# Decay sums of the state-space heads as scanned rows, laid over all partitions through a small DRAM table

## What is computed

```python
da = dtc * a.reshape(G, E)
acs = jnp.cumsum(da, axis=2).transpose(0, 1, 3, 4, 2)
seg = acs[..., :, None] - acs[..., None, :]
lmat = jnp.exp(jnp.where(tri, seg, -jnp.inf))
cb = jnp.einsum('bclgn,bcsgn->bcgls', cc, bc)
y_diag = jnp.einsum('bcgls,bcgels,bcsgep->bclgep', cb, lmat, xdt)
decay_states = jnp.exp(acs[..., -1:] - acs)
states = jnp.einsum('bclgn,bcgel,bclgep->bcgepn', bc, decay_states, xdt)
y_off = jnp.einsum('bclgn,bcgepn,bcgel->bclgep', cc, prev, jnp.exp(acs))
```

## Time and profile before

| what | us |
|---|---|
| median of 3 runs | 1007.55 |
| lowest and highest | 1007.19, 1009.74 |
| the profiled execution | 1008.01 |
| its span, first to last instruction | 1006.2 |
| mean granted PE clock, share of 2.4 GHz | 0.988 |

### The profile page before, as it was taken

One profiled execution on the slowest core, in us unless ns is written; L12 is line 12 of the kernel. 1 busy time (PEld: TensorE's weight loads), 2 busy tenths in 40 slices (PEclk: granted clock), 3 DMA queues, 4 the chain that ended last, 5 costly groups with the idle time before them and its releaser, 6 DMA issues.

```text
span 1006.2 us, 15135 instructions
## 1 busy us (share of the span) xinstructions
PE 962.0 (96%) x6561; PEld 876.1 (87%) x6561; DVE 644.7 (64%) x732; ACT 461.5 (46%) x553; POOL 59.4 (6%) x79
## 2 busy tenths in 40 slices
PE   6999989999999999999899999999899999999996
PEld 6999779999999899776699989997899888999884
DVE  5966895545455853565659778688677765455444
ACT  6456744443435355644454343445354434444342
POOL 2033000000000000120030000000000000000000
PEclk9999999999999999899999999999999999999999
DMA  8743466555564643212479999985455454565621
GB/s 259 242 131 126 159 196 218 180 184 193 175 202 128 188 147 111 84 43 85 153 279 329 387 310 343 306 320 194 172 179 179 145 183 163 176 201 170 204 87 42
DMA packets 122282, 190.52 MB, mean 189 GB/s; under 512 B 6566, under 2 KB 103080, under 8 KB 119144
## 3 DMA queue, kind: packets, MB, share of 16 engines
q1 hardware_dynamic: 115184, 156.94, 48.3%
q0 software_dynamic: 5616, 31.78, 8.6%
q10 hardware_dynamic: 1416, 0.83, 0.3%
HBM read 188.49 MB, written 1.05 MB: 188 GB/s over the span
## 4 chain that ended last, share of the span: by engine, by line
PE 79%; DVE 11%; ACT 6%; issue 2%; DMA 1%; DVEq 0%; ACTq 0%; POOL 0%
PE PS L562 15%; PE PS L564 15%; PE PS L563 15%; PE PS L569 9%; PE PS L570 9%; PE PS L571 9%; DVE lo L1559 4%; ACT hi L1130 2%; PE PS L695 1%; PE PS L660 1%; DMA raw<-even_w_in 1%; ACT hid L1417 1%; DVE r L1629 1%; PE PS L1014 1%; DMA sq<-norm_gains 1%
## 5 line engine op out<-in xcount | busy, mean ns | idle before, releaser
L1559 DVE TENSOR_TENSOR lo<-raw,hi 128x2048 fp32r<-128x2048 f32 (+2 forms) x150 | 336.0, 2259 | 163.8 <-ACT hi L1130 163.5
L562 PE MATMUL PS<-x_hi,hi 128*128 128x256 f32 x1320 | 376.1, 285 | 2.1 <-DVE x_lo L1756 2.1
L564 PE MATMUL PS<-x_hi,lo 128*128 128x256 f32 x1320 | 373.9, 283 | 0.0
L563 PE MATMUL PS<-x_lo,hi 128*128 128x256 f32 x1320 | 373.2, 283 | 0.0
L1130 ACT ACTIVATE hi<-raw 128x2048 fp32r<-128x2048 f32 (+2 forms) x150 | 277.8, 1879 | 8.5 <-DMA raw<-even_w_in 6.4
L562 PEld LDWEIGHTS PS<-x_hi,hi 128*128 128x128 f32 x1320 | 251.9, 191 | 4.5 <-DVE lo L1559 2.4
L563 PEld LDWEIGHTS PS<-x_lo,hi 128*128 128x128 f32 x1320 | 252.7, 191 | 1.7 <-issue 0.5
L564 PEld LDWEIGHTS PS<-x_hi,lo 128*128 128x128 f32 x1320 | 251.8, 191 | 0.0
L569 PE MATMUL PS<-hi,hid_hi 128*128 128x512 f32 x352 | 141.5, 402 | 6.0 <-DVE lo L1559 5.5
L570 PE MATMUL PS<-lo,hid_hi 128*128 128x512 f32 x352 | 139.8, 397 | 0.0
L571 PE MATMUL PS<-hi,hid_lo 128*128 128x512 f32 x352 | 139.1, 395 | 0.0
(11 more groups left out here) (276 smaller groups left out, 833.5 us busy)
## 6 DMA issues: line engine op xcount, KB each, us to landing
raw<-ffn_w_gate SPq DMA_DIRECT2D x22, 1024.0 KB, 5.4
raw<-ffn_w_up SPq DMA_DIRECT2D x22, 1024.0 KB, 5.4
raw<-ffn_w_down SPq DMA_DIRECT2D x22, 1024.0 KB, 5.0
raw<-mlp_w_in SPq DMA_DIRECT2D x16, 1024.0 KB, 5.6
raw<-mlp_w_out SPq DMA_DIRECT2D x16, 1024.0 KB, 5.0
sq<-ada_w POOLq DMA_DIRECT2D x12, 1024.0 KB, 6.2
r<-ada_w POOLq DMA_DIRECT2D x12, 1024.0 KB, 6.7
raw<-sc_w_in SPq DMA_DIRECT2D x12, 1024.0 KB, 5.3
```

What stands on the lines that cost most here:

```text
L562: pe.matmul(dst, wh, hi, start=start, stop=False, skip_group_check=True)
L563: pe.matmul(dst, wh, lo, start=False, stop=False, skip_group_check=True)
L564: return pe.matmul(dst, wl, hi, start=False, stop=stop_, skip_group_check=True)
L1559: dve.tensor_tensor(split_view("lo", c), split_view("raw", c), split_view("hi", c).bitcast(F32), ALU.subtract)\
```

## The change

The running sums are made by DVE, with two scans of 16 x 128 along the rows of the decays, into `small[0:16, 3, :]`. POOL writes these 16 rows to a DRAM tensor `acs_rows` (16 KB) and reads each block's half back onto all 128 partitions, 16 pieces of 512 bytes for each partition, into `r` (block 0) and `lnrow` (block 1). PE's `small` turns the sums instead of the decays, the products L795, L796 and L818 are gone, and DVE and ACT take the sums from the two tiles. The rows of the first layer norm are loaded after the last reader of `lnrow`. The row product of chunk 13 no longer waits for the readers of the PSUM banks.

```diff
+        acs_rows = nc.dram_tensor("acs_rows", (HEADS, S), F32, kind="Internal").ap()
+        acs_all = (r_all[:, :].rearrange("p (h s) -> p h s", h=HEADS),
+                   lnrow[:, :, :].rearrange("p a (b s) -> p (a b) s", s=P))
...
             pool.wait_ge(sem("even_evac"), 1)
             pool.dma_start(pool_w_sb[:, :, :], A["pool_w"][0].rearrange("g c d -> c g d")).then_inc(sem("poolw_landed"), 16)
-            ln_rows("ln0")
+            pool.wait_ge(sem("acs_ready"), 2)
+            pool.dma_start(acs_rows[:, :], small[0:16, 3, :]).then_inc(sem("poolw_landed"), 16)
+            pool.wait_ge(sem("poolw_landed"), 32)
+            for j in range(2):
+                pool.dma_start(acs_all[j], acs_rows[:, j * P:(j + 1) * P].rearrange("(o h) s -> o h s", o=1)
+                               .to_broadcast([P, HEADS, P])).then_inc(sem("acs_landed"), 16)
             pool.wait_ge(sem("pad_zero"), 3)
...
+            pool.wait_ge(sem("seg_done"), 8)
+            pool.wait_ge(sem("eacs_done"), 4)
+            ln_rows("ln0")
             pool.wait_ge(*sig_at("ln0", "x", 4))
...
-                pe.wait_ge(sem("da_ready"), 1)
+                pe.wait_ge(sem("acs_ready"), 2)
...
-                        last = pe.transpose(PS[:, 0, o:o + 16], small[0:16, q, j * P:(j + 1) * P], ident[0:16, 0:16])
+                        last = pe.transpose(PS[:, 0, o:o + 16], small[0:16, 3 * q, j * P:(j + 1) * P], ident[0:16, 0:16])
...
-                    for c in range(2):
-                        pe.matmul(PS[:, 0, 64 + 16 * c:80 + 16 * c], triu, tok[:, c, 16:32], start=True, stop=True)
-                    pe.matmul(PS[:, 0, 96:112], ones[:, :], tok[:, 0, 16:32], start=True, stop=True)\
-                        .then_inc(sem("acs_done"), 1)
...
-                for h in range(HEADS):
-                    last = pe.matmul(PS[:, h // 4, (h % 4) * P:(h % 4) * P + P],
-                                     tok[:, j, 16 + h:17 + h].to_broadcast([P, P]), triu, start=True, stop=True)
...
-                        act.activation(e_acs[:, 4 * q:4 * q + 4, :], PS[:, q, :].rearrange("p (h s) -> p h s", h=4), ACT.Exp)\
+                        act.activation(e_acs[:, 4 * q:4 * q + 4, :], acs_all[1][:, 4 * q:4 * q + 4, :], ACT.Exp)\
...
+            for j in range(2):
+                cols = slice(j * P, (j + 1) * P)
+                dve.tensor_tensor_scan(small[0:16, 3, cols], small[0:16, 1, cols], small[0:16, 1, cols], 0.0, ALU.add, ALU.bypass)\
+                   .then_inc(sem("acs_ready"), 1)
...
-                    dve.tensor_tensor(decay[:, 0, :], neg_acs[:, 0, :], PS[:, 0, 96:112], ALU.add).then_inc(sem("acs_ready"), 1)
+                    dve.wait_ge(sem("acs_ready"), 3)
+                    dve.wait_ge(sem("acs_landed"), 32)
+                    dve.tensor_tensor(decay[:, 0, :], neg_acs[:, 0, :], acs_all[0][:, :, P - 1], ALU.add)\
+                       .then_inc(sem("acs_ready"), 1)
...
-                    dve.tensor_tensor(seg.rearrange("p (h s) -> p h s", h=4), PS[:, q, :].rearrange("p (h s) -> p h s", h=4),
+                    dve.tensor_tensor(seg.rearrange("p (h s) -> p h s", h=4), acs_all[j][:, 4 * q:4 * q + 4, :],
```

More of the change, by code:

```diff
@@ L790, in even_head @@
                 if j == 0:
-                    pe.wait_ge(sem("tok_ready"), 1)
-                    pe.wait_ge(sem("fixed"), 1)
-                    for c in range(2):
-                        pe.matmul(PS[:, 0, 64 + 16 * c:80 + 16 * c], triu, tok[:, c, 16:32], start=True, stop=True)
-                    pe.matmul(PS[:, 0, 96:112], ones[:, :], tok[:, 0, 16:32], start=True, stop=True)\
-                        .then_inc(sem("acs_done"), 1)
-                if j == 0:
                     pe.wait_ge(sem("xbc_ready"), 6)
@@ L807, in even_head @@
                 last.then_inc(sem("xtok_done"), 1)
-            def even_bcast(j):
-                if j == 0:
-                    pe.wait_ge(sem("acs_ready"), 2)
-                    pe.wait_ge(sem("b_tok_ready"), 1)
-                    pe.wait_ge(sem("cb_ready"), 1)
-                else:
-                    pe.wait_ge(sem("seg_done"), 4)
-                for h in range(HEADS):
-                    last = pe.matmul(PS[:, h // 4, (h % 4) * P:(h % 4) * P + P],
-                                     tok[:, j, 16 + h:17 + h].to_broadcast([P, P]), triu, start=True, stop=True)
-                    if h % 4 == 3:
-                        last.then_inc(sem("acs_bcast"), 1)
             def even_state(_):
@@ L852, in even_pool @@
                     pe.wait_ge(sem("pool_diff"), 4)
-                    pe.wait_ge(sem("poolw_landed"), 16)
+                    pe.wait_ge(sem("poolw_landed"), 32)
                 else:
@@ L860, in even_pool @@
                 if i == 1:
-                    pe.wait_ge(sem("seg_done"), 8)
-                    pe.wait_ge(sem("eacs_done"), 4)
+                    pe.wait_ge(sem("tok_ready"), 1)
+                    pe.wait_ge(sem("b_tok_ready"), 1)
+                    pe.wait_ge(sem("cb_ready"), 1)
                     pe.wait_ge(sem("pool_lo_ready"), 1)
@@ L866, in _ @@
             for step, arg in EVEN_STEPS:
-                {"proj": even_proj, "small": even_small, "head": even_head, "bcast": even_bcast, "state": even_state,
+                {"proj": even_proj, "small": even_small, "head": even_head, "bcast": lambda _: None, "state": even_state,
                  "y": even_y, "pool": even_pool}[step](arg)
@@ L1278, in even_head @@
                 if j == 0:
-                    act.wait_ge(sem("acs_ready"), 2)
+                    act.wait_ge(sem("acs_ready"), 4)
                     act.activation(decay[:, 1, :], decay[:, 0, :], ACT.Exp).then_inc(sem("decay_ready"), 1)
@@ L1304, in even_bcast @@
                         if q == 0:
+                            act.wait_ge(sem("acs_landed"), 32)
                             act.wait_ge(sem("pool_diff"), 4)
-                        act.activation(e_acs[:, 4 * q:4 * q + 4, :], PS[:, q, :].rearrange("p (h s) -> p h s", h=4), ACT.Exp)\
+                        act.activation(e_acs[:, 4 * q:4 * q + 4, :], acs_all[1][:, 4 * q:4 * q + 4, :], ACT.Exp)\
                            .then_inc(sem("eacs_done"), 1)
@@ L1774, in _ @@
                .then_inc(sem("da_ready"), 1)
+            dve.wait_ge(sem("da_ready"), 1)
+            for j in range(2):
+                cols = slice(j * P, (j + 1) * P)
+                dve.tensor_tensor_scan(small[0:16, 3, cols], small[0:16, 1, cols], small[0:16, 1, cols], 0.0, ALU.add, ALU.bypass)\
+                   .then_inc(sem("acs_ready"), 1)
             dve.wait_ge(sem("vecs_ready"), 1)
@@ L1807, in even_head @@
                 if j == 0:
[L1808 to L1813 removed]
+                    dve.wait_ge(sem("tok_ready"), 1)
+                    dve.tensor_scalar(neg_acs[:, :, :], tok[:, :, 16:32], -1.0, None, ALU.mult).then_inc(sem("acs_ready"), 1)
+                    dve.wait_ge(sem("acs_ready"), 3)
+                    dve.wait_ge(sem("acs_landed"), 32)
+                    dve.tensor_tensor(decay[:, 0, :], neg_acs[:, 0, :], acs_all[0][:, :, P - 1], ALU.add)\
+                       .then_inc(sem("acs_ready"), 1)
                 dve.wait_ge(sem("xtok_done"), j + 1)
@@ L1834, in even_bcast @@
                 for q in range(4):
-                    dve.wait_ge(sem("acs_bcast"), 4 * j + q + 1)
+                    dve.wait_ge(sem("acs_landed"), 32)
                     if 4 * j + q:
                         dve.wait_ge(sem("exp_done"), 4 * j + q)
-                    dve.tensor_tensor(seg.rearrange("p (h s) -> p h s", h=4), PS[:, q, :].rearrange("p (h s) -> p h s", h=4),
+                    dve.tensor_tensor(seg.rearrange("p (h s) -> p h s", h=4), acs_all[j][:, 4 * q:4 * q + 4, :],
                                       cst("ssm_mask").rearrange("p (o s) -> p o s", o=1).to_broadcast([P, 4, P]), ALU.add)\
```

4 lines of the change are left out of this document (removed).

## The result

| | before | after |
|---|---|---|
| median (6 runs each, on one chip) | 1007.94 us | 1016.55 us |
| lowest and highest | 1006.21, 1009.74 | 1015.03, 1018.51 |
| ratio, with its 95% interval | | 1.0081 [1.0062, 1.0101] |
| the profiled execution | 1008.01 us | 1016.51 us |
| mean granted PE clock | 0.988 | 0.982 |

What follows compares the result with a forecast made beforehand. PE was taken as the bound up to about 103 us; of 7.5 us taken off PE, 2.3 reach the chain, less 1.1 for the clock, a 1.2 us gain: 1006.3 us from a 1007.55 us median, range 1003.4 to 1008.6 us.

Steps and rivals of the forecast that it cites:

- a sign that it was wrong: Second x_dt: expected near 89.6 us; a start later than 91 us (broadcasts or weights) would show the forecast wrong.
- the 0.4 us each: DVE, near 24 us: the two added 16 x 128 scans were taken at 0.4 us each, 0.8 us together.
- I took 1.1: Clock cost of PE's idle time before the second block's rows: up to some 2.2 us, middle 1.1 us taken.
- the sum: 2.3 us gained at the second x_dt (at most 3.1) minus 1.1 us for the clock: 1.2 us gain.
- the drop at 135 us: PE's granted clock at 0.5 from 135 to 138 us in the kernel before, taken to cost 1.6 us.
- rival 1: Clock not hit and additions pass POOL unhindered: 3.1 us gain, 1004.4 us; 1002.8 without the 135 us drop; chance 0.24.
- Step 1: Weight chunks beside the broadcasts: 2 to 3 us later, costing 0 to 1.4 us, counted in the range only.
- Step 2: Block 0's mask additions meeting POOL: three of four at 0.2 to 0.4 us each, 0.6 to 1.2, 0.9 us taken.
- Step 3: PE before the second pool product: a new wait of 1.2 us for the state copy, pool product at 95.9 us.
- one such drop coming: Second pool product, near 96 us: PE waits 4 us for ACT's pool scaling, clock at 0.5 close behind it.
- Rival 3: Broadcasts land late, near 64.5 to 65 us, holding DVE at the decay sum: 3.0 us slower or 1010.0 us; chance 0.10.

Runs made afterwards that it cites:

- 2: Changed kernel without the two broadcasts, their tiles filled by POOL with -1e4 so the decays are zero; 1.0009 of the kernel before.
- 12: Changed kernel without the broadcasts (tiles set to -10000) and with POOL's windows after the fourth mask addition of block 0; 0.9994 of the kernel before.
- experiment 1: Kernel before with the table written and both 1 MB broadcasts loaded but read by nobody, layer-norm rows loaded late; 1.0031 of the kernel before.
- 7: Changed kernel with both broadcasts issued by ACT on its own queue behind its part of projection 3, instead of by POOL; 1.0037 of the kernel before.
- experiment 3: Changed kernel with POOL's windows begun only after the fourth mask addition of block 0; 1.0012 of the kernel before.
- Experiment 5: Changed kernel with the 2 x 16 broadcast products put back on PE at their old places, read by nobody; 1.0012 of the kernel before.
- 4: Changed kernel with block 1's broadcast issued only after block 0's has landed and the sixth projection is evacuated; 1.0050 of the kernel before.
- 11: Changed kernel with late windows, late block 1 broadcast, masked sums and exponentials in place in lmat, projection 12 before the first pool product; 0.9954 of before.
- 9: Kernel before, PE's products kept, with only the in-place edit: masked sums written straight into lmat and the exponential taken in place; 0.9967 of before.

## Why the prediction was wrong

The second x_dt starts at 96.45 us, where the prediction had named anything later than 91 us as a sign that it was wrong.

**What held.** The scans take 0.73 us for two, as the 0.4 us each. The broadcasts landed 10.3 and 13.1 us behind their issue, at 39.5 and 43.5 us, long before the 61 us at which they are read; no wait of DVE stands at the decay sum. PE loses the products, waits 3.6 us for ACT's pool scaling, and the clock falls behind it for a cost of 1.2 us (I took 1.1). Experiments 2 and 12, which have no late chunk, bring the second x_dt forward by 2.45 and 3.4 us and the gated product by 1.1 and 1.6 us, as the sum has it (2.3, at most 3.1; then 1.2 us). So the working holds that far along the chain. The times do not show it: 2 is at 1.0009 and 12 at 0.9994, level with before. One price is not borne out: the drop at 135 us was taken to cost 1.6 us, which rival 1 would get back, but the kernel after has no drop there and stays 5.8 us behind right through.

**Step 1: "A chunk may land 2 to 3 us later ... 0 to 1.4 us, and I count it in the range, not in the sum".** The chunk came 4.5 us late for ACT and made DVE wait 2.2 us; with the 1.2 us of the scans and slowed convolutions, that puts `tok` back by 3.35 us. I had compared the broadcasts with their own deadline, 20 us away, and given the weights a slack that the trace does not have. Before, this load was issued at 34.48 us and landed after 6.8 us, at 41.3, and ACT's part starts at 41.27; DVE's split follows at 44.46 us, 1.3 us behind the end of ACT's part. After, it took 11.3 us. The loads issued from 34 to 35 us, after and before:

```profile
raw<-even_w_in SPq DMA_DIRECT2D x1, 1024.0 KB, 11.3
```

```profile
raw<-even_w_in SPq DMA_DIRECT2D x1, 1024.0 KB, 6.8
```

The queues from 36 to 42 us, first in the kernel after, then before (packets, MB, share of 16 engines):

```profile
q0 software_dynamic: 363, 1.37, 73.9%
q1 hardware_dynamic: 411, 0.42, 23.0%
```

```profile
q1 hardware_dynamic: 1071, 1.08, 60.2%
```

The transfer with 20 us in hand took three quarters of the engines' time, and the weight queue, with none in hand at ACT and 1.3 us at DVE, got 0.42 MB instead of 1.08. By experiment 1 this needs only the traffic, and by 7 it does not hang on POOL's queue.

**Step 2: "at 0.2 us (the row's difference) to 0.4 us each that is 0.6 to 1.2 us".** I took 0.9 us; the two operations took 2.58 us more. My own row had shown an operation of 0.22 us taking 2.27 beside a DVE split: the size of this lock is not a fraction but up to the whole of the other's instruction. I priced it all the same with the mildest row, the lmat product's 1390 against 1214 ns. In experiment 3 the same additions take 0.69 us with POOL moved away, so all of it is POOL. The Trainium skill (SBUF — State Buffer, the section on the physical sides and the shared port pair) says that a DVE operation with two SBUF inputs and a GpSimd operation that reads SBUF exclude each other for a whole instruction; the trace agrees here as well, with POOL's product, held by the split in front of it, at 3.50 instead of 1.89 us, and the forecast should have been priced by it.

**Step 3: "1.2 us is a new wait for the state copy".** Both prices land on the same copy, which comes 4.6 us later, and PE stands ready at 80.0 us instead of 83.0, so the wait is 5.0 us. I had treated PE's idle time as free. It was not: behind it y 0 and the projection ran at 1.2 GHz for 6.8 us and put the second x_dt back by 2.6 us. I had seen one such drop coming, at the pool product, and not asked the question at the other new wait. Experiment 5 shows that this link carries most of the loss: with PE kept busy in front of the copy it goes from 0.58 to 0.81% to 0.12%, with an interval that takes in no loss (1.0012 [0.9991, 1.0033]). In the profile of the kernel after, the clock accounts for 3.8 of the 5.8 us (2.6 and 1.2), and the late copy itself for 2.0. And 2 and 3 show that with one of the prices taken off the wait was 1.6 and 2.4 us, while 4 shows that the lock is enough where PE starts early.

**Rival 3** had the sign but not the mechanism: it wanted the broadcasts at 65 us, and they were there at 43.5. The price of 512-byte pieces that it rests on (134 ns each) was far off; POOL's queue packed them into 544 packets of some 3.9 KB. The slower outcome came through a transfer of somebody else.

**What stays open.** Of the 8.5 us between the profiled executions, 5.8 are traced. The other 2.7 lie where both kernels do the same, in places where the granted clock is low longer in one execution than in the other; what decides that there I have not settled. The traffic alone costs 0.31% (experiment 1), and in the one execution profiled PE does not wait for the state and its clock does not fall before 125 us; so up to 3 us of the loss may have another cause than PE's idle time. That the copy would be harmless at 4.6 us late with PE busy is not shown. Nor is it shown that the scanned rows bring anything on top of the in-place edit: 11 is at 0.9954 and 9 at 0.9967, and their intervals overlap.

## What to carry to other kernels

Work taken off the busiest engine is worth what its next supplier lets it be: before removing it, list each wait that it opens, and look at what the clock does behind a wait of several us, since the loss can exceed the saving. A background transfer has two deadlines, its own and that of the transfers beside it, which may have far less in hand. And where an operand moves from PSUM to SBUF, ask whether GpSimd works at that time, and price the meeting with the longest row, not the shortest.

## What the runs showed of the hardware

- After PE had waited 5.0 to 5.4 us the granted clock was 0.5 for 6.8 us in four of the six places in these profiles, and for 3.4 us in two; after its waits of 2.4 to 3.9 us for the state or the pool operand, for 3.4 us; after those of 0.7 to 1.6 us for the state it did not fall. The length of a wait does not settle it alone: behind waits for weight splits of 1.8 us and then 1.4 us the clock fell at 134.8 us in the kernel before, and behind 1.7 and 1.4 us at the same place in the kernel after it did not. 7 us of products that nobody reads kept the clock full and made the kernel faster than without them (1.0012 against 1.0058 to 1.0081).
- A mask addition of 0.69 us with two SBUF inputs took 2.38 us beside POOL's window product, and that product, begun inside a DVE split, 3.50 instead of 1.89 us.
- Issuing one broadcast of 2048 pieces held POOL for 1.20 to 1.27 us, and DVE products with one SBUF input beside it took up to 1.26 us for two instead of 0.73.
- The same 2 MB of broadcasts moved as 544 packets on POOL's queue, landing in 10.3 and 13.1 us, and as 4128 packets on ACT's, landing in 10.6 and 18.0 us; both held up a weight chunk by about 4 us.
